# The sample tile's products in two 64-column parts of the array, two at a time

## The chip, the cores and the metric

The kernel runs on one core of a Trainium2 chip. The metric is the device time of one execution in microseconds, the median of three runs. TensorE, which multiplies matrices, is PE in the rows (its weight load is PEld), VectorE is DVE, ScalarE is ACT, GpSimd is POOL and SyncE is SP. SP does no arithmetic here; its queue issues most of the transfers. Everything is float32. A product is written as one call in the kernel and appears in the profile as two matmul instructions, so a row's count is twice that of the calls.

## The reference

One step of one decoder layer for 512 prompt tokens and 64 sample tokens (8 sequences of 8), which share all weights. Cut to what matters:

```python
def project(h, w_in):                      # h: (.., 1024); IN_WIDTH = 6656 columns
    z = jnp.einsum('bld,de->ble', h, w_in)
    u, qb, kb, vb, qc, kc, vc, gl = jnp.split(z, cuts, axis=-1)
...
def merge(a, ob, lse, oc, gl, w_b_up, w_c_up, w_out):
    ...
    return (g_a * a + g_b * b + g_c * c) @ w_out
...
def sublayer_pair(x, c, mixer, ...):
    m, new_state = mixer(rms_norm(x, g1) * (1 + sc_m) + sh_m)
    x = x + gt_m * rms_norm(m, g2)
    f = moe(rms_norm(x, g3) * (1 + sc_f) + sh_f, *moe_w)   # 64 experts, top 8, and one shared expert
    x = x + gt_f * rms_norm(f, g4)
    return x, new_state
```

Keys kb and values vb have three groups of 256 columns (one for each dilation 1, 4, 16), kc and vc 128 columns each. The shared expert is `(silu(x @ wg) * (x @ wu)) @ wd` with 256 columns in wg and wu and 1024 in wd.

## The kernel before

The 576 tokens lie in five tiles: four of 128 prompt tokens and tile 4 (`PT_`) with the 64 sample tokens. `parts(t)` is 128 or 64. Where a result has tokens in its rows, the token tile is the stationary operand and the weights are streamed: 8 steps over the 1024 channels, 256 or 512 columns at a time, into one bank of PSUM. For tile 4 only 64 of the 128 columns of the array are used then. These results are called `("k", g, t)`, `("v", g, t)`, `("kvc", t)` (keys and values of the window attention, 256 columns), `("mix", t, h)` (output projection, halves of 512 columns), `("sgu", t)` (gate and up of the shared expert, 512 columns) and `("sy", t, h)` (its down projection, 2 steps).

Each such result is a *fill*. `plan()` lists all fills in order, with a bank for each from a ring of eight, and the engine that empties it ("A" ScalarE, "D" VectorE). TensorE takes them in that order; `bank_for` makes it wait until the fill that had the bank before has been emptied. All engines run hand-written lists in program order, with semaphores between them.

What stands around the change, in order of time:

- Projections u, q, k, v. SP meanwhile issues the writes and reads of two bias tables, then the loads `("in", 4..6)` of the weights. `("in", 6)` goes to the slot of `("in", 3)` and so waits until fill `("k", 2, 4)` is complete. Behind it in the queue stand 20 reads of the bias table `biasP` (line 821), and behind them the writes of `pool_p` and `pool_s` (lines 826 and 827) from the buffer `uouts`, which wait until fill `("uout", 1)` is emptied. Then come the writes of k and v (line 844).
- POOL computes the pooled channels and then issues copies of the caches from DRAM to DRAM (`cache_copy`, lines 1075 and 1077), each of five transfers for one sequence, gated by the start of fills named in `COPY_AT`: the first four by `("k", 0, 0)`, `("k", 2, 0)`, `("v", 0, 0)` and `("v", 2, 0)`.
- Prompt attention: 40 units s with a product `("S", s)`, bias and maximum on DVE (lines 1695, 1699), exponential on ACT (line 1306), transposition `("T", s)` on PE (line 2224), product `("O", s)`. DVE enters it behind a wait for all 20 reads of `biasP`; ACT enters behind a wait for both writes from `uouts`, whose room it overwrites. In units 0 to 12 PE also does q and `kvc` fills beside the units.
- Sample attention, gates, then from `("mix", 0, 0)` on the stage called routing here: `mix` fills, `next_row(t)` on DVE (norm and residual), transposition `h2T`, router `rt`, `routed(t)` on DVE (top 8), `pos`, `place(t)`, `cnt`, `block_of(t)` on DVE, and the shared expert between them on PE, `block_rows(t)` on PE. `block_of(t)` for t of 2 and more waits for `block_rows(t - 2)`.
- The expert loop: 70 blocks of 128 rows, gathered by POOL in four quarter rows each.

## Time and profile before

| | |
|---|---|
| median of 3 runs | 1749.94 us (1745.98 to 1760.59) |
| profiled execution, its own time | 1759.37 us |
| its span, first to last instruction | 1757.5 us |
| mean granted TensorE clock | 0.957 |
| PE busy in matmuls | 1611.5 us (92%) |
| DVE, ACT, POOL busy | 536.8, 298.5, 525.4 us |

A time in the rows is counted from the first instruction of the span. "Idle" in brackets behind a row is the time for which the engine stood still before it, and what ended that. The chain of waits is followed back from the last instruction; a piece with "another core or an unknown queue" is a transfer that it cannot name.

### The profile page before, as it was taken

How to read it: one execution, taken by the hardware profiler on the slowest of the kernel's cores; microseconds unless marked ns; L12 is line 12 of the kernel's file. 1: busy time of each engine (PE TensorE's matmuls, PEld its weight loads, DVE VectorE, ACT ScalarE, POOL GpSimd, SP SyncE). 2: the span in 40 equal slices, each digit the busy share in tenths (PEclk: the TensorE clock that was granted, in tenths of full speed). 3: DMA queues.
4: the chain of work that ended last, by engine and by line, in shares of the span. 5: the costliest groups of instructions: out<-in, count | busy, mean ns of one | idle time of the engine just before them, and what ended most of it. 6: DMA issues, size and time to landing. Idle time of an engine off the chain costs nothing.

```text
span 1757.5 us, 21903 instructions
## 1 busy us (share of the span) xinstructions
PE 1611.5 (92%) x6923; PEld 981.2 (56%) x6924; DVE 536.8 (31%) x979; ACT 298.5 (17%) x747; POOL 525.4 (30%) x660
## 2 busy tenths in 40 slices
PE   3589999799889999999997899999999999999991
PEld 2267888587667777774554344444444444444440
DVE  2330000138531211113695222322222233222224
ACT  2110001227432000001420011111111111111112
POOL 0120060004100000000002555555555555555540
PEclk7689999899889999999999999999999999999996
DMA  9982379705398975107010998999799889999945
GB/s 285 334 279 30 55 270 325 261 5 178 114 283 257 289 264 179 63 1 244 30 73 28 394 345 291 346 342 337 238 336 350 306 283 332 343 338 329 343 142 185
DMA packets 153311, 414.10 MB, mean 236 GB/s; under 512 B 24154, under 2 KB 89638, under 8 KB 127463
## 3 DMA queue, kind: packets, MB, share of 16 engines
q1 hardware_dynamic: 127091, 328.27, 52.8%
q0 software_dynamic: 26160, 84.99, 16.9%
q8 instruction: 42, 0.69, 0.2%
q14 instruction: 18, 0.15, 0.0%
HBM read 395.23 MB, written 99.31 MB: 281 GB/s over the span
## 4 chain that ended last, share of the span: by engine, by line
PE 77%; DMA 12%; SPq 4%; DVE 3%; another core or an unknown queue 1%; issue 1%; POOL 1%; ACT 0%; POOLq 0%; DVEq 0%; ACTq 0%
PE bank L2047 74%; DMA arena<-in_we_down 7%; SPq L727 1%; DMA arena<-in_cache_b 1%; DMA arena<-in_w_in 1%; DMA pscale<-in_pool_scale 1%; PE bank L2224 1%; PE bank L2283 1%; DMA arena<-in_w_ada 1%; PE bank L2604 1%; SPq L709 1%; DMA mods<-arena 1%; PE bank L2073 0%; DVE arena L2037 0%
## 5 line engine op out<-in xcount | busy, mean ns | idle before, releaser
L2047 PE MATMUL bank<-arena 128*128 (+11 forms) x6252 | 1538.1, 435 | 56.6 <-DMA arena<-in_w_ada 26.9
L2047 PEld LDWEIGHTS bank<-arena 128*128 128x128 f32 (+4 forms) x6252 | 898.0, 177 | 632.4 <-issue 500.4
L1145 POOL DMA_INDIRECT arena<-h2rows,icol x288 | 294.2, 1021 | 128.4 <-issue 67.6
L1170 POOL DMA_INDIRECT yacc<-arena,scol x70 | 112.9, 1612 | 207.6 <-DVE arena L2001 172.0
L1990 DVE STREAM_TRANSPOSE arena<-arena 128x1024 f32<-128x1024 f32 x70 | 141.7, 2025 | 18.9 <-DMA arena<-h2rows,icol 18.9
L1995 DVE TENSOR_TENSOR arena<-bank,arena 128x256 f32<-128x256 f32 x70 | 29.7, 425 | 337.5 <-ACT arena L1466 337.5
L1211 ACT ACTIVATE arena<-bank 128x512 f32<-128x512 f32 (+6 forms) x147 | 72.3, 502 | 346.0 <-PE bank L2047 202.7
L1075 POOL DMA_DIRECT2D out<-in_cache_b x24 | 12.2, 517 | 342.8 <-PE bank L2047 342.5
L2001 DVE TENSOR_SCALAR arena<-bank,arena 128x512 f32<-128x512 f32 x70 | 52.5, 751 | 190.9 <-PE bank L2047 190.9
L1466 ACT ACTIVATE arena<-bank 128x256 f32<-128x256 f32 x70 | 26.9, 384 | 447.3 <-PE bank L2047 447.3
L1522 DVE COPY arena<-bank 128x512 f32<-128x512 f32 (+6 forms) x59 | 34.6, 590 | 202.5 <-PE bank L2047 145.2
L1477 ACT ACTIVATE arena<-bank,arena 128x512 f32<-128x512 f32 x70 | 48.1, 687 | 221.5 <-PE bank L2047 221.5
L1344 ACT ACTIVATE arena<-bank 128x288 f32<-128x288 f32 x48 | 19.7, 411 | 219.6 <-PE bank L2047 219.5
L1802 DVE SCALAR_TENSOR_TENSOR arena<-bank,pscale,arena 128x288 f32<-128x288 f32 x16 | 8.3, 518 | 141.0 <-PE bank L2047 140.7
L1161 POOL COPY scol<-arena 128x1 uint32 (+1 forms) x70 | 49.2, 703 | 0.1
L2604 PEld LDWEIGHTS bank<-ident,arena 128*128 128x128 f32 x140 | 27.4, 196 | 34.3 <-issue 32.6
L1141 POOL COPY icol<-arena 128x4 uint32 (+1 forms) x72 | 39.7, 551 | 22.7 <-DVE arena L1977 21.0
L2283 PE MATMUL bank<-ident,arena 128*128 128x128 f32 x216 | 34.7, 312 | 10.8 <-DMA arena<-in_cache_b 6.9
L1695 DVE SCALAR_TENSOR_TENSOR arena<-bank,arena 128x256 f32<-128x256 f32 (+1 forms) x40 | 21.7, 542 | 61.9 <-PE bank L2047 39.5
L1010 POOL TENSOR_TENSOR arena<-arena 128x1024 f32<-128x1024 f32 (+1 forms) x5 | 12.6, 2531 | 91.9 <-DVE arena L1574 91.9
L1053 POOL MEMSET arena<- 128x3840 f32 (+1 forms) x2 | 6.2, 3086 | 104.2 <-PE bank L2047 104.1
L2283 PEld LDWEIGHTS bank<-ident,arena 128*128 128x128 f32 x216 | 27.9, 160 | 16.6 <-issue 13.6
(240 smaller groups left out, 611.8 us busy)
## 6 DMA issues: line engine op xcount, KB each, us to landing
arena<-in_we_gate SPq DMA_DIRECT2D x64, 1024.0 KB, 7.2
arena<-in_we_up SPq DMA_DIRECT2D x64, 1024.0 KB, 10.4
arena<-in_we_down SPq DMA_DIRECT2D x64, 1024.0 KB, 16.4
out<-in_cache_b POOLq DMA_DIRECT2D x8, 4080.0 KB, 17.1
arena<-in_w_ada SPq DMA_DIRECT2D x12, 2048.0 KB, 19.8
arena<-in_cache_b SPq DMA_DIRECT2D x96, 256.0 KB, 5.0
arena<-in_w_in SPq DMA_DIRECT2D x7, 2048.0 KB, 16.8
arena<-in_w_in SPq DMA_DIRECT2D x24, 512.0 KB, 7.0
```

Source lines behind the costliest of these rows:

```text
L1141: pool.tensor_copy(icol[:, 4 * j:4 * j + 4].unsqueeze(1), quads[:, col, :]).then_inc(icol_ready, 1)
L1145: pool.indirect_dma_start(xg[:, j, 256 * g:256 * g + 256], None, quarters, bass.IndirectOffsetOnAxis(ap=icol[:, 4 * j + g:4 * j + g + 1], ...
L1161: pool.tensor_copy(scol[:, j:j + 1], rowtok[:, bass.ds(2 * i + j, 1)]).then_inc(cols_ready, 1)
L1170: pool.indirect_dma_start(yacc[j], bass.IndirectOffsetOnAxis(ap=scol[:, j:j + 1], axis=0), yb[:, j, :], None, bounds_check=TOK - 1, oob_is ...
L1211: act.activation(out, pick(bank), ACT.Copy).then_inc(emptied["A"], 1)
L1477: act.activation(yb[:, j, 0:512], psb[6][:, :], ACT.Copy, scale=wtab[:, cols]).then_inc(y_act, 1)
L1522: dve.tensor_copy(out, pick(bank)).then_inc(emptied["D"], 1)
L1990: dve.transpose(xT[:, j, :].rearrange("p (c g i) -> p c g i", c=KD, g=4), xg[:, j, :].rearrange("p (g i c) -> p c g i", g=4, c=KD)).then_i ...
L2001: dve.tensor_scalar(yb[:, j, 512:1024], psb[7][:, :], wtab[:, cols], None, ALU.mult).then_inc(y_dve, 1)
L2047: return pe.matmul(out, lhsT, rhs, start=first, stop=last)
L2283: ins = pe.transpose(bank[:, n * P:(n + 1) * P], cached("K", kind, b, r, p), ident[:, :])
L2604: ins = pe.transpose(psb[2 + j][:, k * P:(k + 1) * P], act3[:, 3 * j + 2, k:FF:2], ident[:, :])
```

## The change

For tile 4, `by_strips`, `mixed_strips`, `down_strips` and a branch of `shared_in` put two results into the two halves of one bank: partitions 0 to 63 and 64 to 127, each from its own 64 columns of the array, in turn within each step. So two fills of tile 4 become one, or one fill of 256 or 512 columns is streamed as two of half the width. `token_key` says which fill holds what: group 0 of k and group 2 of v are split into 2 x 128 columns, groups 1 and 2 of k share `("k", 2, 4)`, groups 0 and 1 of v share `("v", 1, 4)`. ACT (or DVE in `next_row`) empties such a bank in two instructions. `("mix", 4, 1)` goes away, and `("mix", 4, 0)` with both halves stands ahead of `("rt", 1)`; `("sy", 4, 1)` goes away from behind `("quads",)`. The gathers of quarter rows stand in both kernels.

```diff
+def token_key(kind, g, t):
+
+    if t < PT_:
+        return (kind, g, t)
+    return (kind, {"k": (0, 2, 2), "v": (1, 1, 2)}[kind][g], t)
...
-    for t in (0, 1):
-        out += [("mix", 3 + t, 0), ("rt", t), ("mix", 3 + t, 1)] + turned(t + 1)
+    for t in (0, 1):
+        out += [("mix", 3 + t, 0), ("rt", t)] + mix(3 + t)[1:] + turned(t + 1)
...
-            sp.wait_ge(fills_done, INDEX[("mix", TILES - 1, 1)] + 1)
+            sp.wait_ge(fills_done, INDEX[("mix", PT_, 0)] + 1)
...
+            def strips(key, to):
+
+                bank = wait_fill(act, key)
+                for j, (c, n) in enumerate(sample_cols(key)):
+                    ins = act.activation(to[0:NS, PT_, c:c + n], bank[64 * j:64 * j + 64, 0:n], ACT.Copy)
+                ins.then_inc(emptied["A"], 1)
...
+            def by_strips(key, w, cols, n):
+
+                bank = bank_for(pe, key)
+                for k in range(KD):
+                    for j, c in enumerate(cols):
+                        ins = mm(bank[64 * j:64 * j + 64, 0:n], hT[:, k, SEQ:TOK],
+                                 w[:, 512 * k + c:512 * k + c + n], k == 0, k == KD - 1)
+                close(ins)
...
-                    by_token(("k", g, t), w, (256, 0, 256)[g], t, g > 0)
+                    if t < PT_:
+                        by_token(("k", g, t), w, (256, 0, 256)[g], t, g > 0)
+                    elif g != 1:
+                        by_strips(("k", g, t), w, ((256, 384), None, (0, 256))[g], (P, None, 256)[g])
...
-                    by_token(("v", g, t), w, (0, 256, 0)[g], t, g > 0)
+                    if t < PT_:
+                        by_token(("v", g, t), w, (0, 256, 0)[g], t, g > 0)
+                    elif g != 0:
+                        by_strips(("v", g, t), w, (None, (0, 256), (0, P))[g], (None, 256, P)[g])
...
-                    by_token(key, wait_load(pe, ("in", 6)), 256, key[1], False)
+                    w = wait_load(pe, ("in", 6))
+                    if key[1] < PT_:
+                        by_token(key, w, 256, key[1], False)
+                    else:
+                        by_strips(key, w, (256, 384), P)
...
-                    ins = mm(bank[0:r, :], h2T[:, k, toks(t)], wgu[:, k], k == 0, k == KD - 1)
+                    if t < PT_:
+                        ins = mm(bank, h2T[:, k, toks(t)], wgu[:, k], k == 0, k == KD - 1)
+                        continue
+                    for j in range(2):
+                        ins = mm(bank[64 * j:64 * j + 64, 0:FF], h2T[:, k, toks(t)], wgu[:, k, j], k == 0, k == KD - 1)
...
+            def mixed_strips():
+
+                wo = [wait_load(pe, ("wout", h)) for h in range(2)]
+                bank = bank_for(pe, ("mix", PT_, 0))
+                for m in range(KD):
+                    for h in range(2):
+                        ins = mm(bank[64 * h:64 * h + 64, :], mixT[:, m, SEQ:TOK], wo[h][:, 512 * m:512 * m + 512],
+                                 m == 0, m == KD - 1)
+                close(ins)
```

How it stands on TensorE in the projection of k: from the fill of tile 3 in group 0 to that of tile 4 in group 1 before (rows x columns of a product, times its count).

```order
L2047 MATMUL bank1<-arena 128x256 x8
L2047 MATMUL bank2<-arena 64x256 x8
L2047 MATMUL bank3<-arena 128x256 x8
L2047 MATMUL bank4<-arena 128x256 x8
L2047 MATMUL bank5<-arena 128x256 x8
L2047 MATMUL bank6<-arena 128x256 x8
L2047 MATMUL bank7<-arena 64x256 x8
```

After, from the fill of tile 4 in group 0 to that which holds groups 1 and 2 of tile 4:

```order
L2085 MATMUL bank2<-arena 64x128 x16
L2085 MATMUL bank3<-arena 128x256 x8
L2085 MATMUL bank4<-arena 128x256 x8
L2085 MATMUL bank5<-arena 128x256 x8
L2085 MATMUL bank6<-arena 128x256 x8
L2085 MATMUL bank7<-arena 128x256 x8
L2085 MATMUL bank0<-arena 128x256 x8
L2085 MATMUL bank1<-arena 128x256 x8
L2085 MATMUL bank2<-arena 128x256 x8
L2085 MATMUL bank3<-arena 64x256 x16
```

Group 0 of tile 4 has twice the products at half the width, the fill between groups 1 and 2 is gone, and the last holds twice the products of one before at the same width.

On TensorE in the routing stage, from `("mix", 4, 0)` to `("pos", 0)`, before:

```order
L2047 MATMUL bank5<-arena 64x512 x8
L2047 MATMUL bank6<-arena 128x64 x8
L2047 MATMUL bank7<-arena 64x512 x8
L2073 MATMUL bank0<-ident,arena 128x128 x4
L2073 MATMUL bank1<-ident,arena 128x128 x4
L2047 MATMUL bank2<-arena 128x512 x8
L2047 MATMUL bank3<-arena 128x64 x8
L2047 MATMUL bank4<-arena 128x64
```

and after:

```order
L2085 MATMUL bank5<-arena 64x512 x16
L2085 MATMUL bank6<-arena 128x64 x8
L2111 MATMUL bank7<-ident,arena 128x128 x4
L2111 MATMUL bank0<-ident,arena 128x128 x4
L2085 MATMUL bank1<-arena 128x512 x8
L2085 MATMUL bank2<-arena 128x64 x8
L2085 MATMUL bank3<-arena 128x64
```

Both halves of tile 4's output now stand ahead of the router of tile 1 (the `128x64 x8` row behind them), and nothing stands between that router and the transposition of tile 2.

## Rows read from the trace of the kernel before

**Rows 1.** The page's first line.

```profile
span 1757.5 us, 21903 instructions
```

**Rows 2.** Groups of matmuls by shape, whole span: stationary, streamed, count, busy us, mean.

```profile
L2047 PE MATMUL bank<-arena 128*64 128x256 f32 x112 | 25.7, 382 | 0.0
L2047 PE MATMUL bank<-arena 128*64 128x512 f32 x56 | 25.1, 597 | 0.0
```

**Rows 3.** Timeline of PE around the key scores of the window attention: start, length.

```profile
469.04 1.09 PE L2047 MATMUL bank<-arena 128*64 128x128 f32 x16
470.07 0.33 PE L2283 MATMUL bank<-ident,arena 128*128 128x128 f32 x1
```

**Rows 4.** Chain of waits from the projections to the first prompt unit: start, length.

```profile
107.71 191.17 PE bank L2047 x800
...
304.99 20.13 another core or an unknown queue
...
326.10 1.28 ACT L1306
...
328.42 0.66 PE bank L2224 x2
```

**Rows 5.** Who waited for whom, 295 to 345 us: total, times, longest.

```profile
ACT L1306 <- DVE nmx L1699: 23.4, 1, 23.4
DVE arena L1695 <- DMA arena<-toep: 21.9, 1, 21.9
```

**Rows 6.** Timeline of the SP queue and of POOL, 215 to 326 us.

```profile
217.37 26.80 SPq L714 DMA_DIRECT2D arena<-in_w_in  x3
...
244.21 10.60 SPq L821 DMA_DIRECT2D arena<-toep  x20
...
223.89 1.27 POOL L1041 TENSOR_TENSOR arena<-arena 128x512 f32<-128x512 f32 x1 [101.78 <-DMA mods<-arena]
...
250.87 1.83 POOL L1075 DMA_DIRECT2D out<-in_cache_b  x3 [2.98 <-PE bank L2047]
...
284.38 1.46 POOL L1075 DMA_DIRECT2D out<-in_cache_b  x3 [25.91 <-PE bank L2047]
...
301.42 0.71 SPq L827 DMA_DIRECT2D out<-arena  x1
...
302.41 23.55 SPq L844 DMA_DIRECT2D out<-arena  x14
```

**Rows 7.** DMA queues in 255:272, then 289:307 us: packets, MB, share.

```profile
q0 software_dynamic: 203, 5.46, 90.6%
...
q1 hardware_dynamic: 205, 0.19, 4.8%
...
q0 software_dynamic: 213, 5.66, 93.7%
...
q1 hardware_dynamic: 211, 0.19, 4.3%
```

**Rows 8.** Issue to landing of the 20 reads of line 821, us.

```profile
DMA to landing us min/median/max: 5.0/7.5/70.7
```

**Rows 9.** Chain of waits at the last `kvc` fill, and in the expert loop.

```profile
386.75 5.17 PE bank L2047 x24
...
1014.11 10.30 PE bank L2047 x24
```

**Rows 10.** Timeline of DVE in the routing stage; idle before it in brackets.

```profile
868.26 0.15 DVE L1823 SCALAR_TENSOR_TENSOR stat<-stat 64x1 f32<-64x1 f32 x1 [1.98 <-ACT arena L1387]
...
869.34 0.15 DVE L1825 RECIPROCAL stat<-stat 64x1 f32<-64x1 f32 x1 [0.94 <-ACT stat L1391]
...
895.50 0.19 DVE L1862 TENSOR_SCALAR arena<-arena 64x64 f32<-64x64 f32 x1 [1.30 <-ACT arena L1419]
...
932.37 0.99 DVE L1910 TENSOR_TENSOR arena<-arena 128x800 f32<-128x800 f32 x1 [3.31 <-PE bank L2047]
...
939.54 0.99 DVE L1910 TENSOR_TENSOR arena<-arena 128x800 f32<-128x800 f32 x1 [2.20 <-PE bank L2047]
```

More of the change, by code:

```diff
@@ L172, in mix @@
     def mix(t):
-        return [("mix", t, 0), ("mix", t, 1)]
+        return [("mix", t, h) for h in range(2 if t < PT_ else 1)]
     def turned(t):
@@ L178, in down @@
     def down(t):
-        return [("saT", t), ("sy", t, 0), ("sy", t, 1)]
+        return [("saT", t)] + [("sy", t, h) for h in range(2 if t < PT_ else 1)]
     out = mix(0) + mix(1) + mix(2) + turned(0)
     for t in (0, 1):
-        out += [("mix", 3 + t, 0), ("rt", t), ("mix", 3 + t, 1)] + turned(t + 1)
+        out += [("mix", 3 + t, 0), ("rt", t)] + mix(3 + t)[1:] + turned(t + 1)
     out += [("sgu", 0), ("rt", 2), ("pos", 0)] + turned(3)
@@ L189, in routing_order @@
     last = TILES - 1
-    return out + [("saT", last), ("bexp",), ("sy", last, 0), ("quads",), ("sy", last, 1)]
+    return out + [("saT", last), ("bexp",), ("sy", last, 0), ("quads",)]
 UNITS = ([(k, t, p) for k in (1, 2) for t in range(4) for p in range(2)]
@@ L643, in build @@
         LAST.update({("gate", m): ("gc", m, 1) for m in range(KD)})
-        LAST.update({("wout", h): ("mix", TILES - 1, h) for h in range(2)})
+        LAST.update({("wout", h): ("mix", PT_, 0) for h in range(2)})
         COPY_AT = [("k", 0, 0), ("k", 2, 0), ("v", 0, 0), ("v", 2, 0), ("S", 4), ("ga", 2, 0), ("ga", 4, 0), ("mix", 0, 0)]
@@ L1117, in _ @@
                 cache_copy(b)
-            wait_fill(pool, ("mix", TILES - 1, 1))
+            wait_fill(pool, ("mix", PT_, 0))
             pool.tensor_copy(pick.rearrange("p g (q i) -> p g q i", q=4),
@@ L1258, in _ @@
                 for t in range(0, TILES, 2):
-                    r = parts(t)
-                    empty(("v", g, t), vTM[0:r, t, 256 * g:256 * g + 256], lambda b: b[0:r, 0:256])
+                    if t < PT_:
+                        empty(("v", g, t), vTM[:, t, 256 * g:256 * g + 256], lambda b: b[:, 0:256])
+                    elif token_key("v", g, t) == ("v", g, t):
+                        strips(("v", g, t), vTM)
             act.wait_ge(z_ready, 1)
@@ L1279, in beside @@
                     r = parts(t)
+                    up, c = (0, 128) if t < PT_ else (64, 0)
                     act.activation(kTM[0:r, t, 768:896], bank[0:r, 0:128], ACT.Copy)
-                    ins = act.activation(vTM[0:r, t, 768:896], bank[0:r, 128:256], ACT.Copy)
+                    ins = act.activation(vTM[0:r, t, 768:896], bank[up:up + r, c:c + 128], ACT.Copy)
                 else:
@@ L1396, in mix_norm @@
                 for h in range(2):
-                    bank = wait_fill(act, ("mix", t, h))
-                    squares(junk2[0:r, 512 * h:512 * h + 512], bank[0:r, :], stat[0:r, h, t:t + 1], 3 * t + h)
+                    bank = wait_fill(act, ("mix", t, h if t < PT_ else 0))
+                    up = 0 if t < PT_ else 64 * h
+                    squares(junk2[0:r, 512 * h:512 * h + 512], bank[up:up + r, :], stat[0:r, h, t:t + 1], 3 * t + h)
                 root(stat[0:r, 1, t:t + 1], 2 * t + 2)
@@ L1423, in shared_down @@
                 empty(("saT", t), saT[:, :, 0:r], lambda b: b[:, 0:2 * r].rearrange("p (k n) -> p k n", k=2))
-                for h in range(2):
-                    empty(("sy", t, h), ysh[0:r, t, 512 * h:512 * h + 512], lambda b: b[0:r, :])
+                for h in range(2 if t < PT_ else 0):
+                    empty(("sy", t, h), ysh[:, t, 512 * h:512 * h + 512])
+                if t == PT_:
+                    bank = wait_fill(act, ("sy", t, 0))
+                    for h in range(2):
+                        ins = act.activation(ysh[0:r, t, 512 * h:512 * h + 512], bank[64 * h:64 * h + 64, :], ACT.Copy)
+                    ins.then_inc(emptied["A"], 1)
             def shared_in(t):
@@ L1433, in shared_in @@
                 act.activation(sgat[0:r, 0, :], bank[0:r, 0:FF], ACT.Silu)
-                act.activation(sgat[0:r, 1, :], bank[0:r, FF:2 * FF], ACT.Copy).then_inc(emptied["A"], 1)
+                up, c = (0, FF) if t < PT_ else (64, 0)
+                act.activation(sgat[0:r, 1, :], bank[up:up + r, c:c + FF], ACT.Copy).then_inc(emptied["A"], 1)
             for t in range(3):
@@ L2472, in down_half @@
             def down_half(t, h):
-                r = parts(t)
                 bank = bank_for(pe, ("sy", t, h))
@@ L2477, in down_half, with down_strips @@
                     c = D * k + 512 * h
-                    ins = mm(bank[0:r, :], saT[:, k, 0:r], w[:, c:c + 512], k == 0, k == 1)
+                    ins = mm(bank, saT[:, k, :], w[:, c:c + 512], k == 0, k == 1)
+                close(ins)
+            def down_strips():
+                bank = bank_for(pe, ("sy", PT_, 0))
+                wait_emptied(pe, ("saT", PT_))
+                for k in range(2):
+                    for h in range(2):
+                        c = D * k + 512 * h
+                        ins = mm(bank[64 * h:64 * h + 64, :], saT[:, k, 0:NS], w[:, c:c + 512], k == 0, k == 1)
                 close(ins)
@@ L2535, in _ @@
             turned_rows(0)
-            for t in (0, 1):
-                mixed_rows(3 + t, 0)
-                router(t)
-                mixed_rows(3 + t, 1)
-                turned_rows(t + 1)
+            mixed_rows(3, 0)
+            router(0)
+            mixed_rows(3, 1)
+            turned_rows(1)
+            mixed_strips()
+            router(1)
+            turned_rows(2)
             shared_in(0)
```

46 lines of the change are left out of this document (30 added, 16 removed).

## The prediction

> **What bounds the kernel now.** I read the groups of matmuls first, then the chain of waits, then at each place where the chain leaves TensorE the waits, the queues' timelines and the DMA queues. The span is 1757.5 us [rows 1]. The chain runs on PE without a break through the projections, from 107.71 for 191 us [rows 4]. Then it leaves PE: the first transposition of the attention units, line 2224, begins only at 328.42, behind a transfer of 20.13 us and the first exponential at 326.10 [rows 4]. In the expert loop two blocks take 10.30 us, 24 matmul instructions of 512 columns (429 ns each) for one block, with PE always at work [rows 9]. So whatever starts that loop earlier ends the kernel earlier by as much, and the question is how much of the saved PE time gets that far.
>
> **What the strips cost on PE.** Tile 4 now takes 112 instructions of 256 columns in 25.7 us, 229 ns each, and 56 of 512 columns in 25.1 us, 448 ns each [rows 2]. Both means hold some time for the change into and out of the 64-column form; inside a fill I take 216 ns for 256 columns (half of the 429) and 109 for 128. The trace has one place where two 64-column parts work in turn: 16 instructions of 128 columns start at 469.04, and the next form starts at 470.07 [rows 3]. That is 1.03 us, of which 16 one after the other would need 16 x 0.109 = 1.75. Eight pairs at 0.109 are 0.87, and 0.16 is left for the change of form. So two parts of different data run side by side at the rate of one. I take it that this holds for 256 and 512 columns, where the trace has no pair: a cost for each weight load or switch would show most beside the short 128 columns.
>
> The page TensorEngine Tiling (Array Packing) of the Trainium skill, section Key Properties, says that a change of the tiling mode drains the array, while tiles of one mode load and multiply in parallel. The row agrees with both halves, and by it a switch between the halves costs nothing; if it did cost a drain, the second slow rival below would hold.
>
> Per fill of eight calls, then: 16 x 0.216 = 3.46 us at 256 columns, 1.75 at 128, 6.9 at 512, each with about 0.18 for two changes of form.
> - k: group 0 becomes 2 x 128, saves 1.7. The fill of group 1 goes, saves 3.6. The last keeps its length and holds two. Sum 5.35, all of it ahead of the end of `("k", 2, 4)`.
> - v: the same, 5.35. Together 10.7 us before the end of the projections.
> - kvc: 1.7. mix: 16 x 0.429 and one change, 7.1. sgu: 3.45. sy: 1.8.
> The sum is 24.8 us of PE time. It is not the forecast.
>
> **Projections, 10.7 us, and the stall behind them.** If that stall kept its end, the 10.7 us would be lost in it. So what ends it? DVE waits 21.9 us for the reads of `biasP`, ACT 23.4 us [rows 5], by the code for the maxima and also for the two writes from `uouts`, which are issued at 301.42 [rows 6]. The 20 reads are issued from 244.21 to 254.8, yet the last lands 70.7 us after its issue, against a median of 7.5 [rows 6, 8]. The DMA queues say why. From 250.87 POOL has issued the cache copies; four of them keep the engines busy until about 322. In 255 to 272 us queue q0 (POOL) moves 203 packets with 5.46 MB and q1 (SP) 205 packets with 0.19 MB; in 289 to 307 it is 213 and 211 [rows 7]. Packet for packet, and those of q0 are some 29 times larger. For each copy of about 17.5 us an engine does only 13 packets of SP's queue, whatever stands there.
>
> Now move SP. `("in", 6)` waits for `("k", 2, 4)`: the queue goes on to line 821 at 244.21 [rows 6]. After the change it does so at 238.9, and the last read is issued by 249.5. POOL doesn't move: its work starts at 223.89 on a transfer and its copies follow at 250.87 [rows 6], no fill of k or v is in the way by then, and a copy's data needs some 3 us to begin. Before, about a thousand packets of `biasP` were left when the copies took over; at the rate of some 600 a microsecond ahead of them (2 MB in packets of 0.5 and 1 KB; my count) that is 1.7 us of work. A lead of 5.3 us covers it. All reads land by about 252, and SP's queue is empty when the slow time begins.
>
> The writes from `uouts` are issued 10.7 us earlier, at about 290 to 291. Before, they stood behind some 60 packets per engine, more than the copies' 52 let through, and landed only after the copies' end. Now only they stand there: 79 rows of 2 KB are 5 per engine and each transfer ends with a small packet, 7 in all. At 13 in 17.5 us, with the slow large packets of the third copy first, the seventh is through near that copy's end, at about 306. ACT then needs the 2.3 us from 326.10 to 328.42 [rows 4]: the first transposition comes at 308.4. PE itself gets there at 306.3 (before, its three units and the q fills beside them ended at 317.0). So ACT is late by 2 us, and the stage starts **20.0 us** earlier. The fourth copy's gate opens 9 us earlier (284.38 before [rows 6]), which changes nothing while the third is still running. SP's writes of k and v (14 issues in 23.55 us [rows 6]) stay stuck till the copies end, at the same time as before; their next reader is far behind. What limits the term: below, PE can't be there before 306.3, so at most 22; if the cover is a miss and ACT is released only at the copies' end, the gain is 2 (no `biasP` packets ahead any more). I take the value near the first, since the counts of both windows agree.
>
> On this the page DMA: Bandwidth & Descriptors, section Queues, rings and completion order, gives another rule: an engine drains a whole packet, typically 9 to 17 descriptors, from one ring before it turns to the next. If that held for SP's rows here, the writes would go through in one turn and ACT would be free before PE: 22.1 instead of 20.0, and 1719. It is the fifth case below; the equal counts speak against it, and so does the 70.7 us of a single read.
>
> **kvc, 1.7 us.** The last `kvc` fill lies beside unit 12 in a piece of PE's own chain [rows 9], DVE and ACT wait for PE there, so all 1.7 us count (bounds 0 and 1.9).
>
> **Routing: 7.1 + 3.45 on PE, but DVE is the second bound.** PE is through with tile 4's output 7.1 us earlier, and ahead of the router of tile 1 instead of behind it. DVE can't use all of it. It is busy with `routed(1)` until 866.3, then idle 1.98 and 0.94 us [rows 10] for the squares and a root; the new order has the squares ready, and of the root 0.5 stays: 2.45 us won. From there DVE works almost without a break. Its idle stretches are 1.30 (router of tile 4), 3.31 and 2.20 (`block_rows(0)` and `(1)` on PE) [rows 10]. PE in turn is held by DVE through the banks: `("saT", 0)` has the bank of `("pos", 0)` and `("pos", 2)` that of `("pos", 1)`, in both orders, and DVE empties them only in `place(t)`. By these PE's lead of 7.1 shrinks to 5.0 (it waits for the first until 882.9) and to 4.0 (the second, 898.1). Then sgu adds 3.45: `block_rows(0)` comes 7.45 earlier. DVE meets it 3.75 + 3.31 earlier without idle time, waits for `block_rows(1)` as now, and leaves 7.4 us earlier. I take **7.3 us**; the bounds are 3.75 (only DVE's own) and 10.5 (all of PE's).
>
> **sy, 1.8 us: nothing.** The gathers hang on `("quads",)`, and one fill of the same length as before stands ahead of it; the one behind it only filled the wait for the gather. In the expert loop nothing changes.
>
> **Sum.** 20.0 + 1.7 + 7.3 = 29.0 us. The profiled execution took 1759.37 and would take 1730.4; its time lies 9.4 above the median of 1749.94, and I put the same difference to that: **1720.9 us**, 1.7% less. A difference under 1% either way (17.5 us) is about what a measurement of this kernel can't tell from no change. The three runs before span 14.6 us, perhaps just because the stall ends differently; I don't count on that.
>
> **The cases.**
> 1. As summed: 1721, its own range 1713 to 1731 (routing 3.75 to 10.5; the transposition 306.3 to 314). Chance 0.62.
> 2. The stall's end stays. `uouts` is released only with the copies' end, since the writes need more than 13 packets on some engine or are issued too late for the third copy. For it: in the trace everything of SP's after 255 ends in a cluster at 322 to 326. Against it: that cluster stood behind `biasP`. 2 + 1.7 + 7.3 = 11: 1739. Chance 0.18.
> 3. The halves do not run side by side at 256 and 512 columns. Then PE streams the same columns one after another, and nothing moves but an order: 1750 (1745 to 1755). Only the pair of 128 columns [rows 3] speaks against it. Chance 0.06.
> 4. Slower: each switch between the halves drains the array and nothing overlaps. Price: about 0.09 us (half of the 0.18 above) for each of 104 instructions behind the stall (kvc, mix, sgu 32 each, sy 8), 9.7 us. And the 64 instructions in k make `("k", 2, 4)` end 6 us later than before, so that most of `biasP` falls behind the copies: some 2000 packets more are left at their end, 5 us at 400 a microsecond (my count in the cluster after 322) before ACT and DVE can start. 1765. It decides as soon as the switch isn't free; the pair [rows 3] says it is. Chance 0.05.
> 5. The page's arbitration: 1719. Chance 0.05.
> The rest, 0.04, is what I don't see.
>
> Cases 1 and 5 are faster by over 1%, 2 and 3 within it, 4 about half beyond it, and the rest is split: faster 0.67, same 0.27, slower 0.06. The range 1712 to 1741 holds cases 1, 2 and 5.
>
> **What the changed profile would show.** Tile 4's fills at half their time, a pair of 256-column instructions every 216 ns. The 20 reads landed within 10 us each. The wait of DVE for `toep` gone, the first transposition at 308 and not 328; if it is at 323 or later, case 2. Writes of line 827 landed at 304 to 308. PE waiting about 2 us at `("saT", 0)`, DVE's idle of 3.31 gone. The first block of the expert loop 29 us earlier, and the loop as long as before. I am wrong most easily in the one number 306.

## The result and the profile after

The changed kernel takes **1731.97 us** (median of 4 runs, 1730.76 to 1744.28), the kernel before beside it 1753.48 us (4 runs, 1745.98 to 1760.59). The ratio is 0.9866, 95% interval 0.9818 to 0.9914: 21.5 us or 1.3% less, where 29.0 us and 1720.9 us were forecast. The profiled execution of the changed kernel took 1732.06 us, 27.3 less than that of before (1759.37).

The page's first line:

```profile
span 1730.1 us, 22031 instructions
```

The groups of matmuls by shape that hold tile 4's products, over the whole span (count, busy us, mean ns; the last also holds the key scores of the window attention):

```profile
L2085 PE MATMUL bank<-arena 128*64 128x256 f32 x96 | 11.0, 382 | 0.0
...
L2085 PE MATMUL bank<-arena 128*64 128x512 f32 x40 | 10.8, 691 | 0.0
...
L2085 PE MATMUL bank<-arena 128*64 128x128 f32 x128 | 8.8, 279 | 0.0
```

An instruction of 256 columns now takes 11.0 / 96 = 0.115 us of PE, against 0.229 before [rows 2], one of 512 columns 0.27 against 0.448. From start to end a single one is no shorter than before (382 ns as before, and 691 against 597), because two are in flight together; it is the busy time of the group that tells that they run side by side.

The chain of waits of the changed kernel from the projections to the first attention units (start, length), which answers to [rows 4]:

```profile
107.83 178.66 PE bank L2085 x832
...
288.19 0.35 SPq L842
...
289.01 14.63 DMA out<-arena
...
303.66 0.89 ACT arena L1334 x4
...
304.69 0.41 PE bank L2281 x2
```

The piece on PE is 12.5 us shorter. The transfer in this chain is now the second write from `uouts`, 14.63 us. ACT starts 0.02 us after it has landed, and the first transposition begins at 304.69, not 328.42. The transfer of 20.13 us before [rows 4] was another one. It ended at 325.12, and behind it the chain of before goes over DVE, not straight to ACT:

```profile
325.14 0.44 DVE arena L1695
```

DVE had waited there for the reads of `biasP` [rows 5]. In the second trace of before, further down, the chain names the transfer:

```profile
319.40 3.81 DMA arena<-toep
```

So before, the reads of `biasP` came last, and after, with these out of the way, the write. Of the waits from 272 to 320 us in the changed kernel, those that answer to [rows 5]:

```profile
ACT arena L1334 <- DMA out<-arena: 8.8, 1, 8.8
...
ACT L1334 <- DVE nmx L1734: 3.3, 1, 3.3
```

DVE waits for no read of `toep` any more. The SP queue and POOL, 205 to 320 us, beside [rows 6]:

```profile
214.25 23.11 SPq L730 DMA_DIRECT2D arena<-in_w_in  x3
237.41 10.54 SPq L837 DMA_DIRECT2D arena<-toep  x20
288.19 0.35 SPq L842 DMA_DIRECT2D out<-arena  x1
289.01 0.72 SPq L843 DMA_DIRECT2D out<-arena  x1
290.00 28.12 SPq L860 DMA_DIRECT2D out<-arena  x14
...
219.16 1.27 POOL L1057 TENSOR_TENSOR arena<-arena 128x512 f32<-128x512 f32 x1 [98.28 <-DMA mods<-arena]
...
246.02 1.83 POOL L1091 DMA_DIRECT2D out<-in_cache_b  x3 [2.86 <-issue]
```

The reads begin 6.8 us earlier. The forecast held POOL fixed, but here its copies begin 4.85 us earlier too, since the transfer that POOL waits for came at 219.16 instead of 223.89. No edit touches that transfer, and over the traces of this study the first copy begins anywhere from 242.1 to 259.3 us. The queues in 289:307 us, packets and MB, beside the second pair of [rows 7], and issue to landing of the 20 reads, beside [rows 8]:

```profile
q0 software_dynamic: 210, 5.72, 93.9%
q1 hardware_dynamic: 193, 0.25, 3.8%
```

```profile
DMA to landing us min/median/max: 4.1/6.2/40.7
```

Still nearly packet for packet. At least one of the reads was caught by the early copies (40.7 us for the worst, where 10 us at most was forecast), but all had landed before DVE wanted them.

In the routing stage, PE's waits for DVE from 840 to 935 us, and from DVE's timeline the two places in `block_of(2)` and `block_of(3)` where it stood idle for 3.31 and 2.20 us before [rows 10]:

```profile
PE bank L2085 <- DVE arena L1952: 2.1, 2, 1.6
PE bank L2526 <- DVE arena L1925: 1.6, 1, 1.6
PE bank L2085 <- DVE arena L1925: 1.0, 1, 1.0
```

```profile
904.35 0.99 DVE L1948 TENSOR_TENSOR arena<-arena 128x800 f32<-128x800 f32 x1
...
910.47 0.99 DVE L1948 TENSOR_TENSOR arena<-arena 128x800 f32<-128x800 f32 x1 [1.56 <-PE bank L2085]
```

The second row of the waits is the one at `("saT", 0)`, the third that at `("pos", 2)`. Before, these two were not there, and the first was, with the same 2.1 us. DVE's idle time of 3.31 us is gone, as forecast, and that of 2.20 us is 1.56.

**Where the 27.3 us are.** For each execution with a trace I took the start of the last matmul of some fills. The columns: from the first `u` fill to the first transposition `T(0)`; what of it lies behind `kT(5)`, the last of the transposed keys, where the projections are over; attention units 26 to 39; from the end of the output gates to `rows(3)`; from there to `quads`. `rows(3)` stands for `("rows", 3)`, and so on. The last column is the time of the first transposition in the expert loop. All in us.

| kernel | u to T(0) | kT(5) to T(0) | O(26) to O(39) | gates to rows(3) | rows(3) to quads | first expert block |
|---|---|---|---|---|---|---|
| before, profiled | 214.3 | 26.5 | 36.6 | 153.0 | 8.2 | 975.8 |
| before, again | 212.8 | 24.9 | 41.4 | 151.6 | 8.2 | 974.3 |
| after, profiled | 191.7 | 15.0 | 42.2 | 146.2 | 11.4 | 950.1 |
| after, again | 193.5 | 16.9 | 43.8 | 146.2 | 11.4 | 953.2 |

So the step to T(0) gained 22.6 us in these two executions (20.0 forecast) and the routing 6.8 to `rows(3)`. Two places gave something back: 5.6 us between O(26) and O(39), and 3.2 before the quads. There the granted clock stood differently. The windows of these two stretches, first of after, then of before (start:end, length, busy times of PE, its loads, DVE, ACT and POOL, then the granted clock, DMA share, GB/s):

```profile
399.20:441.40 42.20, 36.32 (x211) 29.13 (x209) 28.41 (x86) 26.39 (x91) 11.59 (x14) 0.88 0.19 64
921.40:927.60 6.20, 6.20 (x23) 2.52 (x23) 2.04 (x11) 1.11 (x3) 0.00 (x0) 0.56 0.00 0
```

```profile
424.70:461.40 36.70, 31.68 (x211) 25.67 (x209) 26.81 (x86) 26.30 (x91) 11.61 (x14) 1.00 0.25 79
949.80:953.50 3.70, 3.70 (x20) 1.96 (x19) 2.33 (x14) 0.87 (x2) 0.00 (x0) 1.00 0.00 0
```

The same 211 matmuls, at 1.00 of the clock before and 0.88 after, which is a mix of its two levels, 2.4 and 1.2 GHz. In the second stretch the mean of 0.56 is nearly all at the low level. Whether this belongs to the change is a question for the experiments.

### The profile page after: what moved, and what is told of

The parts are those of the page before. It is cut to its first block, busy times and chain, and to the rows that moved or that the text cites. A ratio compares the mean times of both kernels' runs of the same rounds, so it can differ in the third digit from the quotient of the medians.

```text
span 1730.1 us, 22031 instructions
## 1 busy us (share of the span) xinstructions
PE 1591.4 (92%) x6987; PEld 976.2 (56%) x6988; DVE 539.4 (31%) x979; ACT 299.1 (17%) x749; POOL 522.0 (30%) x660
## 4 chain that ended last, share of the span: by engine, by line
PE 78%; DMA 10%; DVE 5%; SPq 4%; issue 1%; POOL 1%; ACT 1%; POOLq 0%; DVEq 0%; ACTq 0%
PE bank L2085 75%; DMA arena<-in_we_down 5%; SPq L743 1%; DMA arena<-in_cache_b 1%; PE bank L2281 1%; DMA pscale<-in_pool_scale 1%; PE bank L2340 1%; DMA out<-arena 1%; PE bank L2684 1%; DMA arena<-in_w_ada 1%; DMA mods<-arena 1%; SPq L725 1%; POOL arena L1026 0%; DVE arena L1576 0%; SPq L779 0%
## 5 line engine op out<-in xcount | busy, mean ns | idle before, releaser
L2085 PE MATMUL bank<-arena 128*128 (+10 forms) x6316 | 1516.5, 433 | 55.4 <-DMA arena<-in_w_ada 24.4
L1227 ACT ACTIVATE arena<-bank 128x512 f32<-128x512 f32 (+5 forms) x139 | 69.1, 506 | 310.3 <-PE bank L2085 162.6
L1372 ACT ACTIVATE arena<-bank 128x288 f32<-128x288 f32 x48 | 19.7, 410 | 219.7 <-PE bank L2085 219.6
L1334 ACT ACTIVATE arena<-arena,nmx 128x128 f32<-128x128 f32 (+1 forms) x80 | 35.0, 439 | 13.9 <-DMA out<-arena 8.8
```

Source lines behind the costliest of these rows:

```text
L1227: act.activation(out, pick(bank), ACT.Copy).then_inc(emptied["A"], 1)
L1334: ins = act.activation(v, v, ACT.Exp, bias=nmx[:, s % 4, h:h + 1], accum_out=den[:, s % 4, h:h + 1])
L2085: return pe.matmul(out, lhsT, rhs, start=first, stop=last)
```

## The experiments

Times are medians. Each ratio is to the kernel before in runs on the same chip, whose median was between 1753.5 and 1756.1 us in every set.

**1. The sample tile's k and v strips alone.** The kernel before with this part of the change and none of the others:

```diff
-                    by_token(("k", g, t), w, (256, 0, 256)[g], t, g > 0)
+                    if t < PT_:
+                        by_token(("k", g, t), w, (256, 0, 256)[g], t, g > 0)
+                    elif g != 1:
+                        by_strips(("k", g, t), w, ((256, 384), None, (0, 256))[g], (P, None, 256)[g])
```

> The kernel before with the sample tile's k and v strips alone; kvc, mix, sgu and sy stay as before. My theory (the strips bring the uouts writes forward by what TensorE saves, and the wait at T(0) for them moves with them, by more than the 10.7 us saved because fewer of the writes' packets stand beside the cache copies): T(0)'s bank opens at 305 to 309 us instead of 328.7, the whole kernel gains 17 to 23 us, and the routing stage is as long as before. Rival (the wait at T(0) is set by the copies, which do not move): T(0) stays at 326 to 329 and the gain is 0 to 3 us. Rival (most of what was measured comes from the routing stage): gain 10 to 12 us, what TensorE alone saves.

1737.92 us, ratio 0.991 (0.9874 to 0.9945). `u` to T(0) is 192.8 us, with `kT(5)` to T(0) 16.2, and T(0) opens at 306.1. Gates to `rows(3)` 151.6, as in the second trace of before. So the two strips of k and v carry the whole stall term, at 20.0 to 21.5 us of trace. The first rival is out by T(0), and so is the second, which had nothing but TensorE's own time. By the ratio the gain is 15.8 us, 1.2 below the expected range, in an interval of 9.7 to 22.1. Which of the two it was that helped, the strips of k ahead of the reads of `biasP` or those of v ahead of the writes of `uouts`, was not tried apart.

**2. All of the change but k and v.** The changed kernel with k and v of tile 4 as before:

```diff
-                    elif g != 1:
-                        by_strips(("k", g, t), w, ((256, 384), None, (0, 256))[g], (P, None, 256)[g])
+                    by_token(("k", g, t), w, (256, 0, 256)[g], t, g > 0)
```

> The changed kernel with k and v of the sample tile as before; kvc, mix, sgu and sy by strips. My theory: T(0) as before at about 328, the gain is kvc 1.7 and routing 6.9 to 7.4, less what the clock takes back, 5 to 9 us in all. Rival (the sum of the parts is not additive, since time won in routing is lost before the expert loop): gain 0 to 3 us.

1749.92 us, ratio 0.9967 (0.9941 to 0.9994): about 5.8 us, the low end of what was expected. `u` to T(0) 213.8, as before; gates to `rows(3)` 147.9, to `quads` 8.2. The gains of experiments 1 and 2, 15.8 and 5.8 us by their ratios, make 21.6 together, and the whole change gave 21.5. The parts add as far as such intervals can tell (each of the three is 5 to 8 us wide on either side).

**3. and 4. The copies late, before and after.** Is it really the copies that make T(0) late? The first four wait until the second attention unit's scores are closed (`cache_copy` waits for the end of the fill that `COPY_AT` names, not for its start):

```diff
-        COPY_AT = [("k", 0, 0), ("k", 2, 0), ("v", 0, 0), ("v", 2, 0), ("S", 4), ("ga", 2, 0), ("ga", 4, 0), ("mix", 0, 0)]
+        COPY_AT = [("S", 1), ("S", 1), ("S", 1), ("S", 1), ("S", 4), ("ga", 2, 0), ("ga", 4, 0), ("mix", 0, 0)]
```

> The kernel before with its first four cache copies held back until the second attention unit's scores are closed, so that no copy stands beside the bias reads or the uouts writes. My theory (the 11 to 12 us beyond TensorE's work before T(0) are the uouts writes sharing the DMA engines with the copies): T(0) opens at 316 to 319 us instead of 328.7, with no strips at all, and the gain is 9 to 12 us if the copies, now later, disturb nothing. Rival (the writes take that long by themselves): T(0) at 328, gain 0. Rival (late copies stand beside the cache loads of the key stage): T(0) at 317, but the gain is lost by the end of the attention stage, 0 or slower.

> The changed kernel with the same late copies. My theory: T(0) at 302 to 304 us, where TensorE's own work ends, so only 1 to 3 us better than the changed kernel (28 to 30 us below the profiled kernel before, 22 to 25 below the median); together with the other three it says how much of the change is TensorE's work and how much the shared DMA engines. Rival (late copies collide with the cache loads): slower than the changed kernel by 5 us or more.

In the kernel before: 1748.08 us, ratio 0.996 (0.9935 to 0.9985). Its chain of waits, and the landing of the 20 reads of line 821:

```profile
302.91 11.57 PE bank L2047 x44
314.49 0.37 PE bank L2224 x2
314.86 5.01 PE bank L2047 x20
...
403.63 5.24 DMA out<-arena
```

```profile
DMA to landing us min/median/max: 4.1/5.6/7.9
```

PE runs from the scores into the transposition without a wait, and T(0) stands at 314.6; `kT(5)` to T(0) is 13.2 us instead of 26.5 and 24.9. So 11.7 to 13.3 us of the old path were the copies, and with no copy beside them no read takes over 7.9 us (70.7 before [rows 8]). That part of the theory is shown. But the median gained only 7.3 us, where 9 to 12 were expected: the chain goes over a write for 5.24 us at 403.63, and O(26) to O(39) takes 45.1 us. Line 833 issued that write. It is one of the last four of new keys and values, for which DVE waits before it takes the outputs of unit 24; the write and read back of the combine come only behind it. The copies don't stand beside it. In 403:409 us the queues moved:

```profile
q1 hardware_dynamic: 2121, 1.81, 94.4%
q0 software_dynamic: 41, 0.03, 2.7%
```

It is late since SP's queue was late. Ahead of it stand SP's loads of the caches, which now lie beside the copies, and their issues take 62.48 and 21.83 us:

```profile
315.36 62.48 SPq L722 DMA_DIRECT2D arena<-in_cache_b  x1
377.88 21.83 SPq L727 DMA_DIRECT2D arena<-in_cache_b  x8
```

In the kernel before, the same issues take 0.58 and 3.95 us, and SP comes to the last four writes at 391.35 instead of 399.82. So the last rival, copies beside the cache loads, had the right cause, though it cost a part of the gain and not all of it.

In the changed kernel: 1735.3 us, ratio 0.9877 (0.984 to 0.9914), no better than without. T(0) gains nothing worth the name (191.5 from `u`, at 306.0 where 302 to 304 was expected; `kT(5)` to T(0) is 14.9 us with a fall of the clock in it). The chain pays 5.99 us at the same write:

```profile
394.85 5.99 DMA out<-arena
```

The copies have to be done somewhere, and either `uouts` or the loads ahead of the last writes of k and v then share the DMA engines with them.

**5. and 6. Both kernels once more.** Is the clock in the light stretches chance or change?

> The changed kernel itself once more, with a second trace. Theory (the granted clock in the light stretches between 400 and 420 us and before the quads falls or holds by how each execution happens to stand to it): the windows at 1.2 GHz stand elsewhere in this trace, and the time from O(26) to O(39) is anywhere between 36.7 and 43.8 us. Rival (they belong to the change): the same windows, 42 us, and the same 3 us before the quads. The median should be 1732 to 1738 us.

> The kernel before itself once more, with a second trace. By the theory of chance its time from O(26) to O(39) need not be 36.7 us again; five other traces had 42 to 48. By the rival it is 36.7 us again, with no window at 1.2 GHz there. T(0)'s wait should be 10 to 13 us beyond TensorE's own work in both. Median 1750 to 1757 us.

After: 1736.26 us, ratio 0.9908 (0.9879 to 0.9938). Before: 1754.05 us, ratio 1.0003. Both second traces are in the table above. The kernel before now takes 41.4 us from O(26) to O(39), at a clock of 0.88, where its first trace had 36.6:

```profile
423.50:465.00 41.50, 36.46 (x211) 29.28 (x210) 27.02 (x86) 26.20 (x91) 11.60 (x14) 0.88 0.20 67
```

So the 5.6 us "lost" there are mostly a lucky execution of before. It is the only one of the ten traces up to experiment 8 without a fall of the clock there; experiment 11 has 36.6 us once more. For the changed kernel itself, experiment 5 expected the falls in other places, and that did not come true: its second trace has them within 0.4 us of where the first has them, counted from O(26) and from the gates, and again 11.4 us before the quads, where before has 8.2 twice. That was the rival's sign. It does not hold up over all traces: those of experiments 4 and 11, with the same routing stage, have 8.2.

**7. The output product of tile 4 in two banks again, in the old order.**

```diff
-            mixed_strips()
-            router(1)
-            turned_rows(2)
+            mixed_rows(4, 0)
+            router(1)
+            mixed_rows(4, 1)
+            turned_rows(2)
```

> The changed kernel with the sample tile's output product (mix of tile 4) in two banks, one half after the other, in the order of before. My theory: the pair saves 3.45 us of TensorE and 3.1 us of wait before rt(2), of which 2.8 us are given back at saT(0) and pos(2) as TensorE waits for DVE; undone, the routing stage loses 3.7 to 4.1 us, so its gain falls from 6.9 to about 3. Rival (the order, not the strips, made the gain): no more than 3.45 us lost at rt(2). Rival (nothing of it reaches the end): same routing end as the changed kernel.

1731.56 us, ratio 0.9896 (0.9853 to 0.994): as fast as the changed kernel. Gates to `rows(3)` is 148.2 us, 2.0 more than with the strips, but `rows(3)` to `quads` is 8.2, 3.2 less. Up to `rt(2)` the strips are 6.6 us ahead. After PE's wait of 1.6 us for DVE, `saT(0)` is 4.9 ahead, and `pos(2)` only 2.0. Between these two the clock falls in every trace that has these strips, for 3.4 or 6.8 us; of the five traces with the old order only the first of before has such a fall in that place. But the fall doesn't decide it: `pos(2)` stands 106.9 to 107.0 us behind the gates in all seven traces with these strips and the old banks, however long the fall. There PE waits for DVE, which is the bound. What was expected (3.7 to 4.1 us lost) is wrong: **the largest of the strips, 7.1 us of PE time, bring 2.0 us to `rows(3)` and none that can be seen in the median.** From the gates to the quads this kernel takes 156.4 us. The traces with all strips of this stage, the old banks and no fall of the clock before the quads take 154.5 (that of experiment 2, with one fall more elsewhere, 156.2), and those with the fall 157.6 or 157.7.

**8. The shared gate and up product of tile 4 over all 512 columns again.**

```diff
-                    for j in range(2):
-                        ins = mm(bank[64 * j:64 * j + 64, 0:FF], h2T[:, k, toks(t)], wgu[:, k, j], k == 0, k == KD - 1)
+                    ins = mm(bank[0:r, :], h2T[:, k, toks(t)], wgu[:, k], k == 0, k == KD - 1)
```

> The changed kernel with the sample tile's shared gate and up product as one product over all 512 columns. My theory: it loses 3.1 to 3.45 us at sgu(4) and no more, the routing gain falls from 6.9 to 3.5. Rival (the wait for DVE at rows and quads takes it up): 0 to 1 us lost.

1737.37 us, ratio 0.9899 (0.9862 to 0.9937). Gates to `rows(3)` is 149.6 us, 3.4 more: all of the 3.45 of PE counts there. (`rows(3)` to `quads` is 9.8 us, with a shorter fall of the clock.) The medians can't tell it apart.

**9. Other banks for two fills.** PE waits for `place(0)` and `place(1)` only because of the banks that the ring hands out:

```diff
+    at = {k: n for n, (k, _, _) in enumerate(fills)}
+    for a, b in ((("pos", 0), ("h2T", 3, 0)), (("pos", 1), ("h2T", 4, 1))):
+        (ka, wa, na), (kb, wb, nb) = fills[at[a]], fills[at[b]]
+        fills[at[a]], fills[at[b]] = (ka, wa, nb), (kb, wb, na)
     return fills
```

> The changed kernel with two exchanges in the list of banks: pos(0) with h2T(3,0), and pos(1) with the second half of h2T(4), so that saT(0) and pos(2) are written into banks that ScalarE empties early, not DVE's place(0) and place(1). My theory: TensorE's waits of 1.6 us at saT(0) and 1.0 us at pos(2) go, and with the first of them the fall of the clock at sy(0); rows(3) closes 2.6 to 4.1 us earlier counted from the end of the output gates, 1728 to 1733 us as a median. Rival (DVE is the bound of this stretch and the wait only moves, to cnt or to the rows): 0 to 1 us at rows(3).

1730.59 us, ratio 0.9888 (0.9853 to 0.9923). PE's waits from 840 to 935 us in this kernel:

```profile
PE bank L2089 <- DVE arena L1956: 2.1, 2, 1.6
PE bank L2089 <- DVE arena L1929: 1.7, 1, 1.7
```

The wait of 1.6 at `saT(0)` did not go: it moved one fill on, to `sy(0, 0)`, which now has the bank of `pos(0)` (1.7). Only the 1.0 at `pos(2)` is gone. Gates to `rows(3)` is 145.3 us, 0.9 less, and not 2.6 to 4.1. The fall of the clock at `sy(0)` is still there; before the quads it is 8.2 us, without a fall. So the rival was right about the first wait, and the median doesn't separate this kernel from the changed one.

**10. Two copies early, two late.**

```diff
-        COPY_AT = [("k", 0, 0), ("k", 2, 0), ("v", 0, 0), ("v", 2, 0), ("S", 4), ("ga", 2, 0), ("ga", 4, 0), ("mix", 0, 0)]
+        COPY_AT = [("k", 0, 0), ("k", 2, 0), ("S", 1), ("S", 1), ("S", 4), ("ga", 2, 0), ("ga", 4, 0), ("mix", 0, 0)]
```

> The changed kernel with two of the first four cache copies where they were and the other two after the second attention unit's scores. My theory: the first two are done before the uouts writes start at about 289 us, T(0) opens at 303 to 304 us (in a kernel whose first product of u ends at 113 us) with no wait for a write, and the last two are done before the combine's write at about 392 us, so that nothing is paid there, as it was with four late copies (6 us). Gain over the changed kernel 1 to 3 us. Rival (the split copies push the last two into the combine's write all the same): 2 to 6 us lost at O(30).

1726.69 us, ratio 0.9857 (0.9815 to 0.9899). The profiled execution was an odd one (span 1735.4): the transfers ahead of the copies were so late that PE waited 4.1 us for a weight in the v stage and the first copy began at 259.29. So T(0) came at 310.4 and not at 303 to 304. Even so no write is waited for at T(0) (14.9 us behind `kT(5)`, all of it PE's, with a clock below full in it), and no 6 us are paid at the last writes of k and v (what was expected calls them the combine's), which SP issues from 369.73 on (O(26) to O(39) is 41.2 us). The interval overlaps both of the changed kernel, so a gain over it isn't shown.

**11. The strips of k, v and kvc one half after the other.** The same instructions; only their order differs:

```diff
-                for k in range(KD):
-                    for j, c in enumerate(cols):
+                for j, c in enumerate(cols):
+                    for k in range(KD):
```

> The changed kernel; of k, v and kvc of the sample tile the eight products of one half of the array now stand in a row and then the eight of the other half, instead of one of each in turn. Same instructions, same banks, same readers. My theory (the saving is two neighbouring products in the two halves running at once): k and v of tile 4 take as long as before the change (10.3 us less saved, 55.3 us from k(2,4) to v(2,4) instead of 49.8), and the kernel is 11 to 20 us slower than the changed one, since T(0)'s wait comes back too. Rival (a product needs only half the time because it writes 64 columns): as fast as the changed kernel. Rival (the engine looks further ahead than one instruction and overlaps the two rows anyway): in between.

1745.46 us, ratio 0.9947 (0.9916 to 0.9978): by the ratios 7 to 14 us slower than the two measurements of the changed kernel. The groups by shape, 180 to 300 us, of the changed kernel and then of this one:

```profile
L2085 PE MATMUL bank<-arena 128*64 128x256 f32 x64 | 7.3, 382 | 0.0
...
L2085 PE MATMUL bank<-arena 128*64 128x128 f32 x64 | 3.9, 276 | 0.0
```

```profile
L2085 PE MATMUL bank<-arena 128*64 128x256 f32 x64 | 12.6, 382 | 0.0
...
L2085 PE MATMUL bank<-arena 128*64 128x128 f32 x64 | 6.7, 276 | 0.0
```

11.2 us against 19.3 us for the same 128 instructions. The pairing is in the neighbourhood of the queue, not in the width of a product; the rival of the half-price product is out. But 3.1 us of the 11.1 saved to the end of v are kept. In the trace of single instructions the second half of a fill starts at 200.84 us while the last one of the first half starts only at 201.16: the engine does look ahead to the other half, by a few instructions. So the third prediction holds, in between. The stall is back as well: `kT(5)` to T(0) is 25.1 us, 8.2 more than in the changed kernel's second trace, and the chain waits for the write from `uouts`:

```profile
295.45 24.60 DMA out<-arena
```

This is the prediction's second case, come true in another kernel. The copies' last packets are over at 319.7 us, and the write lands at 320.05, with them. In the six traces with the strips of k and v and early copies it was issued 6 to 10 us earlier and landed 14 to 16 us earlier.

**12. Both repairs together.**

> The changed kernel with both repairs, the exchanged banks in the routing stage and the two cache copies put behind the second unit's scores. If the two add up: T(0) without a wait for a write (17 to 18.5 us behind v(2,4)), O(30) not later than O(26) by more than 14 us, no wait at saT(0), 6 to 8 us gained between the output gates and the quads, and a median of 1722 to 1728 us. Rival (the clock takes back what the waits gave): 1728 to 1736 us, no better than the changed kernel.

**1723.96 us**, 6 runs from 1718.97 to 1730.72, ratio 0.9826 (0.979 to 0.9862), span 1717.2. It lies within what was expected. It is the fastest of the study, and its interval lies below the changed kernel's second measurement (0.9879 to 0.9938) though it overlaps the first. Its chain at T(0), its queue of SP, and the window before the quads:

```profile
290.95 11.57 PE bank L2089 x44
302.53 0.37 PE bank L2285 x2
302.90 5.01 PE bank L2089 x20
```

```profile
288.62 0.72 SPq L847 DMA_DIRECT2D out<-arena  x1
289.61 8.55 SPq L864 DMA_DIRECT2D out<-arena  x14
```

```profile
911.60:915.30 3.70, 3.70 (x24) 1.98 (x23) 2.30 (x14) 1.02 (x3) 0.00 (x0) 1.00 0.00 0
```

`kT(5)` to T(0) is 13.2 us, PE's own work and nothing else (16.8 us behind `v(2,4)`, 0.2 below the range); the 14 issues of SP's writes take 8.55 us instead of 28.12, since no copy stands beside them. Gates to `rows(3)` is 144.5 us, to `quads` 8.2, together 7.0 less than in the second trace of before.

## Why the prediction was right in most parts, and its gain 7.5 us too large

**Two products at once.** Right. 0.115 us an instruction of 256 columns, where 0.108 with a change of form on top was forecast; to the end of v 11.1 us were saved (10.7 forecast). Cases 3 and 4, no overlap or a drain at each switch, are out by the first trace; experiment 11 shows what no overlap costs.

**The stall.** Right in size, and in its two causes: the reads of `biasP` were out of the way before DVE wanted them, and the write from `uouts` then landed before the copies' end. Forecast: T(0) 20.0 us earlier, 9.3 of it from the stall. Measured from `u`, the two traces of before average 213.5 us; the six with the k and v strips, copies where they were and all other timing alike (the two of after, experiments 1 and 7 to 9) average 193.9, so 19.7. The place where I said I was most easily wrong, the landing of `uouts` at 306, came out at 303.66. It was not by a better rule of the queue but since the copies themselves began 4.85 us earlier in that execution. Over all six the write landed between 303.6 and 305.8 us, though it was issued anywhere from 285.6 to 289.4, while the copies moved data from 249 to 253 until 317 to 321. That is near the end of the third of four copies, as the prediction had it, and so a write issued earlier gained nothing more. Counted from `u`, T(0) came 1.1 to 4.3 us later in the other five than in the first. The term has a spread of its own, which the sum did not carry: the first copy's start wanders by some 17 us.

Case 5 took up the page DMA: Bandwidth & Descriptors of the Trainium skill, section Queues, rings and completion order, by which an engine drains a whole packet, typically 9 to 17 descriptors, from one ring before the next. By that `uouts` could have gone through in one turn. The counts in 289:307 us are 210 to 193, and the write took 14.63 us. What the traces count as packets takes turns nearly one for one, and case 5 is out. Whether such a packet is what the page means by one, the traces don't tell.

**kvc, 1.7 us.** Not contradicted: T(0) to O(26) is 96.1 and 96.8 us before, 95.7 with the k and v strips alone, and 94.3 and 95.4 with all strips. That is 0.3 to 2.5 us, by which pair one takes, so its size is open.

**sy, nothing.** It was not tried apart; nothing in the traces speaks against it.

**Routing, 7.3 us: the step that was off.** Up to `rows(3)` the profiled pair gives 6.8, but before's first trace had a short fall of the clock there of its own. Against the 151.6 us that three traces of the old order share, the changed order gives 5.4, of which 2.0 belong to mix and 3.4 to sgu. The waits that were forecast at `saT(0)` (2.1) and `pos(2)` (1.0) were there, with 1.6 and 1.0, and sgu was right (3.45 forecast). The term that was too large is the lead that PE keeps at `pos(2)`: 4.0 forecast, 2.0 measured against the traces of before's order without that fall. The working took its times from before's first trace, in which the fall had put `pos(2)` 1.5 us later, and left the clock out.

The clock then took more before the quads. In four of the nine traces with the mix strips it falls there (11.4 us twice, 11.5 and 9.8, against 8.2 in the other five), in none of the five without them. The count speaks for the strips as the cause but doesn't show it. To the quads the changed kernel's two traces give 2.2 us in place of 7.3.

**What else went.** The expert loop is about as long as before: 781.7 and 781.6 us from its first block to the end of the span before, 780.0 and 778.4 after, and 777.8 to 782.7 over all fourteen traces. Added up from `u` to the quads, the second traces of the two kernels give 19.3 us to T(0), 1.4 to O(26), -2.4 to O(39), 0.6 in the stage of the cached keys and up to the gates' end, and 2.2 in the routing: 21.1. That this is near the 21.5 of the medians is in part luck, since the same two spans differ by 24.3 us, 3.2 of it in the expert loop. The forecast time missed by 11 us, since it also started low: it hung on the median of three runs, 1749.94, while five sets of runs put the kernel before at 1753.5 to 1756.1.

**A slip in the text.** It says that in the expert loop two blocks take 10.30 us; the row has one block of 24 instructions in that time, as the same sentence goes on to say. No number of the sum used it. In case 4, 104 times 0.09 us is 9.4 and not 9.7; its 1765 stays.

## What to carry to other kernels

When TensorE gets faster in front of a wait, ask what ends the wait: here 11 us of products were worth 20, because the reads and writes that they released no longer met as many packets of a background copy. When such a copy is moved, look at every transfer that stands in line behind the ones it now meets. Where another engine is nearly the bound, saved TensorE time turns into waits for it; undo such a part alone before keeping it, as the largest of these strips shows. And a single profiled execution may be the lucky one: take a second trace of the kernel before, ahead of explaining a loss in a stage that the change doesn't touch.

## What the runs showed of the hardware that I had not expected

- TensorE overlaps products of the two 64-column halves also when they stand a few instructions apart in its queue: with eight and eight in a row, 3.1 us of the 11.1 were still saved, and the second half's first instruction started 0.32 us before the first half's last.
- Small transfers beside a large copy between places in memory go nearly packet for packet (193 to 210 in 289:307 us), and the queue that issues them is held up: 14 issues of writes took 28.12 us with the copies beside them and 8.55 us without, the issue of one cache load 62.48 us against 0.58.
- Falls of the granted clock in one and the same stretch of the program come and go between executions of one kernel: 36.6 and 41.4 us for the same 211 matmuls.
